# Slot numbers and slot scatters of a mixture-of-experts layer, given out token tile by token tile

## What is computed

```python
def routed_experts(h, idx, w, w_e1, w_e3, w_e2):
    t, d = h.shape
    n = t * TOP_K
    flat_e = idx.reshape(n)
    ...
    order = jnp.argsort(flat_e)
    se, stok, sw = flat_e[order], flat_tok[order], flat_w[order]
    counts = jnp.bincount(flat_e, length=N_EXPERTS)
    padded = (counts + EXPERT_BLOCK - 1) // EXPERT_BLOCK * EXPERT_BLOCK
    ...
    dest = pad_start[se] + (jnp.arange(n) - start[se])
    ...
    xd = jnp.zeros((n_rows, d), h.dtype).at[dest].set(h[stok])
    ...
    return jax.ops.segment_sum(yd * wd[:, None], td, num_segments=t)

def moe_ffn(h, lw):
    scores = jax.nn.sigmoid(h.astype(jnp.float32) @ lw['w_router'].astype(jnp.float32))
    ...
    return routed + swiglu(h, lw['w_s1'], lw['w_s3'], lw['w_s2'])
```

## Time and profile before

| | us |
|---|---|
| median of 3 runs | 1769.77 (1768.54 to 1770.4) |
| the profiled execution | 1767.64, span 1765.8 |
| block A | 776.5 to 876.3 |
| block B | 876.3 to 960.8 |
| TensorE busy | 1562.3 (88% of the span), mean granted clock 0.954 |
| VectorE busy | 1007.9 (57%) |
| ScalarE busy | 728.2 (41%) |
| GpSimd busy | 653.8 (37%) |

### The profile page before, as it was taken

The page is one execution under the profiler, slowest core; times in us unless marked ns, Lnnn a source line. Parts: engine busy times, 40 slices in busy tenths (PEclk is TensorE's granted clock), DMA queues, the critical chain, the costliest instruction groups (busy, mean ns, idle before and its releaser), DMA issues. The chain is left out here.

```text
span 1765.8 us, 22716 instructions
## 1 busy us (share of the span) xinstructions
PE 1562.3 (88%) x7699; PEld 1181.3 (67%) x7699; DVE 1007.9 (57%) x1578; ACT 728.2 (41%) x1067; POOL 653.8 (37%) x727
## 2 busy tenths in 40 slices
PE   7799787788889999999892999999999999999990
PEld 2688687688879998964541666666666666666660
DVE  1956677656665466526552666555555555555644
ACT  2423343333342131102212566555565555656650
POOL 0533474422213332310055345444444444444540
PEclk9999899889989999999896999999999999999995
DMA  9320100000015465444163899999999999999944
GB/s 320 96 93 3 37 1 1 1 1 1 1 47 150 139 204 177 135 148 158 72 263 128 290 357 374 351 344 341 345 348 347 339 344 345 342 332 341 339 149 181
DMA packets 129672, 352.50 MB, mean 200 GB/s; under 512 B 21316, under 2 KB 77256, under 8 KB 102600
## 3 DMA queue, kind: packets, MB, share of 16 engines
q1 hardware_dynamic: 97880, 237.71, 36.9%
q10 hardware_dynamic: 10288, 71.86, 11.1%
q0 software_dynamic: 21440, 42.08, 9.5%
HBM read 335.16 MB, written 47.87 MB: 217 GB/s over the span
## 5 line engine op out<-in xcount | busy, mean ns | idle before, releaser
L2247 DVE TENSOR_TENSOR e_wlo<-mem,e_whi 128x2048 fp32r<-128x2048 f32 x140 | 314.6, 2288 | 119.8 <-ACT e_whi L2187 119.8
L2187 ACT ACTIVATE e_whi<-mem 128x2048 fp32r<-128x2048 f32 x140 | 260.3, 1908 | 36.0 <-PEq L1847 23.6
L2157 PE MATMUL psum<-mem 128*128 128x512 f32 x560 | 252.0, 593 | 1.5 <-ACT mem L2219 1.5
L2137 PE MATMUL psum<-e_whi,e_xhi 128*128 128x512 f32 x560 | 228.2, 407 | 7.1 <-DVE e_xlo L2254 7.1
L2094 POOL TENSOR_TENSOR held<-nhalf 1x1 f32<-1x1 f32 x206 | 126.2, 613 | 284.5 <-DMA sums<-mem_h,si 118.6
L2139 PE MATMUL psum<-e_wlo,e_xhi 128*128 128x512 f32 x560 | 222.3, 397 | 0.0
L2138 PE MATMUL psum<-e_whi,e_xlo 128*128 128x512 f32 x560 | 222.2, 397 | 0.0
L2157 PEld LDWEIGHTS psum<-mem 128*128 128x128 f32 x560 | 101.0, 190 | 102.2 <-issue 102.1
L1481 POOL TENSOR_TENSOR w_lo<-mem,w_hi 128x1024 fp32r<-128x1024 f32 x30 | 76.8, 2581 | 161.3 <-ACT w_hi L1425 161.3
L2254 DVE TENSOR_TENSOR e_xlo<-psum,e_xhi 128x512 fp32r<-128x512 f32 x140 | 90.2, 686 | 77.8 <-ACT e_xhi L2193 77.8
L927 ACT ACTIVATE mem<-psum,small 128x640 f32<-128x640 f32 (+1 forms) x80 | 60.3, 754 | 175.6 <-DVE small L1096 107.2
(11 more groups left out here) (313 smaller groups left out, 3309.5 us busy)
## 6 DMA issues: line engine op xcount, KB each, us to landing
mem<-in_w_e SPq DMA_DIRECT2D x144, 1024.0 KB, 12.4
mem<-in_w_e ACTq DMA_DIRECT2D x66, 1024.0 KB, 11.2
mem<-in_w_mod SPq DMA_DIRECT2D x24, 1024.0 KB, 12.5
mem<-in_w_in SPq DMA_DIRECT2D x16, 512.0 KB, 4.5
mem<-in_w_in SPq DMA_DIRECT2D x3, 2048.0 KB, 8.9
sums<-mem SPq DMA_DIRECT2D x10, 512.0 KB, 16.6
mem<-sums SPq DMA_DIRECT2D x10, 512.0 KB, 7.8
mem<-in_x_sample SPq DMA_DIRECT2D x8, 512.0 KB, 11.4
```

The costliest lines, as they stand in the source:

```text
L2137: pe.matmul(out, xh, wh, start=first, stop=False)
L2157: mm = pe.matmul(pY[:, cs], gT[:, f, :], w2[v][:, f, cs], start=(f == 0), stop=(f == 1))
L2187: act.activation(wHi13[u % 2][:, a], w13[u][:, a], ACT.Copy).then_inc(se["h13"], 1)
L2247: dve.tensor_tensor(wLo13[u][:, a], w13[u][:, a], wHi13[u % 2][:, a].bitcast(F32), ALU.subtract)\
```

## The change

Slot numbers no longer wait for the counts of all tiles. Blocks beyond the first of an expert are given out in the order in which they come up, tile by tile: `over[t]` holds how many such blocks each expert has after t tiles, `cur` where its newest is, `owner` who owns which. Per tile there are now five steps: `place` (TensorE: positions, and counts so far), `blocks_of` (VectorE: which experts need a new block), `ranks` (TensorE: in which order they get one), `new_blocks` (VectorE) and `spread` (TensorE: broadcasts the three columns to all rows), then `slots_of` (VectorE) and `scatter_slots` (GpSimd). For tiles 0 to 2 the numbers are made in block A, and the scatters of tiles 0 and 1 are issued there, between GpSimd's norm steps; tiles 3 and 4 are numbered in B, and tiles 2 to 4 scattered there. The output projection is cut in halves, with `place` between them. In B, SyncE's load of the third expert's second weights (`load_w2(SH - 1)`, 1 MB) moves behind the slot numbers, since their scratch memory lies in that buffer, and ahead of the load of the slot table.

```diff
+    def place(pe, t):
+        pe.wait_ge(s_sel, t + 1)
+        if t:
+            pe.wait_ge(s_k8, 2 * t)
+        for a in range(t + 1):
+            mm = pe.matmul(pPos, tri if a == t else ones, sel[:, a, :], start=(a == 0), stop=(a == t))
+        if t:
+            for a in range(t + 1):
+                mm = pe.matmul(pCnt, sel[:, a, :], ones[:, 0:1], start=(a == 0), stop=(a == t))
+        mm.then_inc(s_pos, 1)
+    def ranks(pe, t):
+        pe.wait_ge(s_bcol, t)
+        pe.matmul(pRank, triX, flag, start=True, stop=False)
+        pe.matmul(pRank, ones[0:NE, 0:NE], over[t], start=False, stop=True).then_inc(s_rank, 1)
+    def spread(pe, t):
+        pe.wait_ge(s_diag, t)
+        pe.matmul(bank(7)[:, 128:128 + 3 * NE], ones[0:NE, :], diag.rearrange("p a e -> p (a e)"),
+                  start=True, stop=True).then_inc(s_bc, 1)
+    def blocks_of(dve, t):
+        chain = Chain(dve, s_rv, route_chain[0])
+        dve.wait_ge(s_pos, t + 1)
+        chain(dve.tensor_scalar(over[t + 1], pCnt, float(P), None, ALU.is_gt))
+        for a in range(2, t + 1):
+            chain(dve.scalar_tensor_tensor(out=over[t + 1], in0=pCnt, scalar=float(P * a), in1=over[t + 1],
+                                           op0=ALU.is_gt, op1=ALU.add))
+        dve.tensor_tensor(flag, over[t + 1], over[t], ALU.subtract).then_inc(s_bcol, 1)
+    def new_blocks(dve, t):
+        dve.wait_ge(s_rank, t)
+        ...
+        for n, v in enumerate((over[t], cur, step1)):
+            ins = dve.tensor_scalar(diag[:, n, :], ident[0:NE, 0:NE], v, None, ALU.mult)
+        ins.then_inc(s_diag, 1)
+        ...
+    def slots_of(dve, t):
+        dve.wait_ge(s_pos, t + 1)
+        if t == 0:
+            dve.wait_ge(s_rec, 16)
+            chain(dve.scalar_tensor_tensor(out=gsel, in0=pPos, scalar=float(NBLK), in1=enum, op0=ALU.mult, op1=ALU.add))
+        else:
+            dve.wait_ge(s_bc, t)
+            ...
+        chain(dve.scalar_tensor_tensor(out=gsel, in0=gsel, scalar=1.0, in1=sel[:, t, :], op0=ALU.add, op1=ALU.mult))
+        chain(dve.max(k8[:, t, :], gsel))
+        ...
+    def scatter_slots(pool, t, part):
+        pool.wait_ge(s_tin, 16)
+        pool.wait_ge(s_k8, 2 * (t + 1))
+        for n in range(t * TOPK + part[0], t * TOPK + part[1]):
+            pool.indirect_dma_start(out=S["slots"], ...
@@ block A, TensorE
             for t in range(1, NT):
-                out_proj(t)
+                out_proj(t, 0)
+                if t >= 2:
+                    place(pe, t - 2)
+                out_proj(t, 1)
+                if t >= 3:
+                    ranks(pe, t - 2)
                 turn(t - 1)
                 router(t - 1)
+                if t >= 3:
+                    spread(pe, t - 2)
@@ block A, GpSimd
                 pool.tensor_tensor(RS2, RS1, nhalf[:, 0:1], ALU.pow).then_inc(sr["rs"], 1)
+                if t == 2:
+                    scatter_slots(pool, 0, (0, 4))
+                if t == 3:
+                    scatter_slots(pool, 0, (4, 8))
+                    scatter_slots(pool, 1, (0, 4))
+                if t == 4:
+                    scatter_slots(pool, 1, (4, 8))
@@ block A, VectorE
                 dve.tensor_tensor(x1[:, t, :], x1[:, t, :], xres[t % 2], ALU.add).then_inc(sr["x"], 1)
+                if t >= 3:
+                    new_blocks(dve, t - 2)
...
                 if 1 <= t < NT - 1:
                     select(dve, t - 1)
+                if t >= 2:
+                    slots_of(dve, t - 2)
+                if 2 <= t < NT - 1:
+                    blocks_of(dve, t - 1)
                 dve.wait_ge(sr["T"], t + 1)
@@ block B, SyncE
                 load_w13(sp, u, u)
-                load_w2(sp, u, u)
+                if u < SH - 1:
+                    load_w2(sp, u, u)
...
+            sp.wait_ge(s_k8, 2 * NT)
+            sp.wait_ge(s_er, 1)
+            load_w2(sp, SH - 1, SH - 1)
             sp.wait_ge(s_tsc, 16 * NT * TOPK)
@@ block B, TensorE (counts, place and block sums of all tiles go)
+            place(pe, 3)
             turn(0)
+            pe.wait_ge(sh["g"], 1)
+            up(1, 0, 2)
+            ranks(pe, 3)
+            up(1, 2, 4)
+            spread(pe, 3)
+            up(1, 4, KT)
+            down(0)
+            turn(1)
+            pe.wait_ge(sh["g"], 2)
+            place(pe, 4)
...
+            pe.wait_ge(s_own, 1)
+            pe.wait_ge(s_k8, 2 * NT)
+            pe.matmul(pOwn, pnum[0:NE, :], owner, start=True, stop=True)
+            pe.matmul(pNb, over[NT], ones[0:NE, 0:1], start=True, stop=True).then_inc(s_er, 1)
+            down(1)
+            turn(2)
@@ block B, VectorE
             dve.memset(xg[1], 0.0).then_inc(s_zero, 1)
+            product(0)
+            blocks_of(dve, 3)
             dve.wait_ge(s_hp, 16 * NT)
             select(dve, NT - 1)
...
+            new_blocks(dve, 3)
+            slots_of(dve, 3)
+            product(1)
+            blocks_of(dve, 4)
+            new_blocks(dve, 4)
+            dve.sem_inc(s_own, 1)
+            slots_of(dve, 4)
             dve.memset(xg[0], 0.0).then_inc(se["z"], 1)
```

More of the change, by code:

```diff
@@ L1591, in up_bank @@
     def up_bank(t):
-        return bank(7 if t == 0 else 0)
+        return bank(2 if t == 0 else 0)
+    RT = M_SC + 7168
+    qv, isn, blkv, gsel = (mem.at(RT + NE * n, NE) for n in range(4))
+    eqb = mem.at(RT + 256, TOPK * NE)
+    diag = mem.at(RT + 256, 3, NE, rows=NE)
+    k8 = mem.at(RT + 768, NT, TOPK)
+    w8 = mem.at(RT + 808, NT, TOPK)
+    owner = mem.at(RT + 848, NE, rows=NE)
+    over = [small[0:NE, 4 + t:5 + t] for t in range(NT + 1)]
+    cur, flag, rank1, step1, mine = (small[0:NE, 10 + n:11 + n] for n in range(5))
@@ L1665, in _, with out_proj @@
             pe.wait_ge(s_wout, 16 * KT)
-            def out_proj(t):
-                if t >= 2:
+            def out_proj(t, half=None):
+                if t >= 2 and half != 1:
                     pe.wait_ge(sr["x"], 2 * (t - 2) + 2)
-                for c in range(2):
+                for c in range(2) if half is None else (half,):
                     for k in range(KT):
@@ L1740, in _ @@
             dve.wait_ge(s_cst, 16)
+            chain = Chain(dve, s_rv, route_chain[0])
+            dve.memset(over[1], 0.0)
+            dve.memset(owner, 0.0)
+            chain(dve.tensor_copy(cur, pnum[0:NE, :]))
+            route_chain[0] = chain.n
             for t in range(NT):
@@ L1874, in turn, with up @@
                 tr.then_inc(sh["T"], 1)
+            def up(t, k0, k1):
+                for k in range(k0, k1):
+                    mm = pe.matmul(up_bank(t).rearrange("p (a n) -> p a n", a=2), h2T[:, k, t * P:(t + 1) * P],
+                                   w13[SH][:, :, k, :], start=(k == 0), stop=(k == KT - 1))
+                if k1 == KT:
+                    mm.then_inc(sh["h"], 1)
             def down(t):
@@ L1938, in _ @@
         def _(pool):
[L1939 to L1946 removed]
+            for t in range(2, NT):
+                scatter_slots(pool, t, (0, TOPK))
             pool.wait_ge(s_tab, 16)
@@ L1977, in _ @@
-            for a in range(2, NT):
-                chain(dve.scalar_tensor_tensor(out=oblk, in0=cnt, scalar=float(P * a), in1=oblk,
-                                               op0=ALU.is_gt, op1=ALU.add))
-            dve.tensor_scalar(oblkb, ones[0:NE, :], oblk, None, ALU.mult).then_inc(s_ob, 1)
-            dve.wait_ge(s_pos, 1)
-            chain(dve.tensor_copy(posv, bank(4)[:, 0:NT * NE].rearrange("p (t e) -> p t e", t=NT)))
-            chain(dve.tensor_scalar(jv, posv, float(P), None, ALU.is_ge))
@@ L1985, in _ @@
-            for a in range(2, NT):
-                chain(dve.scalar_tensor_tensor(out=jv, in0=posv, scalar=float(P * a), in1=jv,
-                                               op0=ALU.is_ge, op1=ALU.add))
-            chain(dve.scalar_tensor_tensor(out=posv, in0=jv, scalar=-float(P), in1=posv, op0=ALU.mult, op1=ALU.add))
-            dve.wait_ge(s_os, 1)
-            chain(dve.tensor_copy(rt[:, 2880:3008], bank(6)[:, 0:2 * NE]))
-            chain(dve.tensor_tensor(ostart, ostart, enum, ALU.subtract))
```

138 lines of the change are left out of this document (50 added, 88 removed).

## The result

The changed kernel takes 1784.82 us (median of 4 runs, 1783.1 to 1785.78) where the kernel before takes 1769.15 beside it (4 runs): a ratio of 1.0087, 95% interval 1.0073 to 1.0102. Slower by 0.9%, 1.5 us under the forecast of 1786.3. Its profiled execution took 1784.27 us (span 1782.5), against 1767.64.

What follows compares the result with a forecast made beforehand. Block B was taken as bound by GpSimd's scatters, block A not. A's +29.0 us less B's 12.5 gave +16.5 us: 1784.1 for the profiled execution, 1786.3 for the median, range 1774 to 1794.

Steps and rivals of the forecast that it cites:

- -12.5 forecast: Block B (slot numbers, slot scatters, shared expert): 12.5 us shorter, bounds 11.7 to 14.7, as the slot table lands earlier.
- +29.0 forecast: Block A (output projection, norm, router, choice of experts): 29.0 us longer from TensorE's stands, added matmuls and lost clock.
- stand at place(0): Middle of out_proj(2) in block A: TensorE waits 2.7 us for tile 0's selection.
- stand at place(1): Middle of out_proj(3) in block A: TensorE waits 6.6 us for tile 0's slot numbers, 17.1 against 10.6.
- stand at place(2): Middle of out_proj(4) in block A: TensorE waits 6.0 us for tile 1's slot numbers, 19.0 against 13.0.
- stands at spread: Behind the router in block A: spread(1) and spread(2) each wait 1.5 us for new_blocks, 3.0 us.
- item 6: Block A: half clock in projection halves behind the three place stands, 5.1 us (bounds 0 to 5.1); spread's stands cost nothing.
- (a): Block A: stands cost no clock, small matmuls run at full clock too; +9.8 us, 1779.6; chance 0.12.
- (b): Fourth turn of block A: scatters hold VectorE up, 3.9 us more; +20.4 us, 1790.2; chance 0.05.
- (c): Block A: the two long stands do not occur, VectorE's chain being quicker; no change, 1768.7; chance 0.08.
- (d): Block A: TensorE stands for no new step, grows 4.0 us by matmuls alone; -8.5 us, 1761.3; chance 0.10.
- (e): Block B: table load waits longer for the shared expert, gain only some 8 us; +21 us, 1790.8; chance 0.05.

Runs made afterwards that it cites:

- table_before_w2: Changed kernel with SyncE loading the slot table ahead of the moved 1 MB weight load: 1783.31 us, ratio 1.0083.
- scatter_in_b: Changed kernel with all 40 scatters issued in block B, slot numbers of tiles 0 to 2 still made in A: 1783.3 us, ratio 1.0088.
- order: Changed kernel with only TensorE's queue reordered: place behind the whole projection, ranks behind the transposition, both spreads moved later: 1759.4 us, ratio 0.9951.
- spread_later: Changed kernel with only the two spreads moved, into out_proj(4) and the shared expert's first product: 1785.33 us, ratio 1.0091.
- early_release: Changed kernel with place waiting only for VectorE's last read of the PSUM bank, not for the slot numbers: 1775.79 us, ratio 1.0042.
- before_again: The kernel before, unchanged, traced a second time: 1780.99 us, beside runs where the kernel before took 1781.33.
- all_scatters_b: The kernel of order_table_early with all 40 scatters issued in block B: 1781.97 us, ratio 0.9997; run again 1780.26 us, ratio 0.9994.
- order_table_early: The kernel of order with SyncE's table load and moved weight load ahead of the stores of tiles 2 and 3: 1753.9 us, ratio 0.9917.
- before_waits: The kernel before with only three TensorE waits for the selection added, in the middle of out_proj(2), (3) and (4): 1775.92 us, ratio 1.0038.

## Why the prediction was right, and where it was not

**B (-12.5 forecast, -13.1 measured).** The steps held one by one: the scatters ended 16 us before the load (17 forecast), the load was issued 56.1 us into B (56.5), it took 2.8 us longer than before (the forecast left 0 to about 3 open and took 2.4; `table_before_w2` puts 1.95 of it on the weight load), and the gathers behind it were unchanged. The drain, costed as before, was 0.65 us shorter, which is why B gained 13.1 and not 12.5. Which part brings the gain was left unsaid: `scatter_in_b` shows that it is the slot numbers done early, and not the sixteen scatters.

**A (+29.0 forecast, +31.4 measured).** By term, from the TensorE rows above:

| us | forecast | measured |
|---|---|---|
| stand at place(0) | 2.7 | 1.06 |
| stand at place(1) | 6.6 | 6.52 |
| stand at place(2) | 6.0 | 4.48 |
| stands at spread | 3.0 | 2.49 |
| matmuls of place, ranks, spread | 5.6 | 6.3 |
| clock | 5.1 | 7.2 |
| joins and the first turn of A | 0 | 3.4 |

place(1) was right because its chain was: from the end of out_proj(2) to the slot numbers the trace gives 823.74 to 840.92, 17.2 us, and I had 17.1. place(0) and place(2) were mis-sized for the same reason, TensorE being late by itself: the first half ahead of place(0) took 8.46 instead of 7.08, and the half ahead of place(2) 8.47. What TensorE loses to the clock ahead of a wait it gets back at the wait: in the trace of `table_before_w2` the half ahead of place(2) takes 9.87 and the stand is 2.98, together 12.85, where the kernel after has 8.47 + 4.48 = 12.95.

The step that failed is item 6, the clock, which came out at 7.2 us, above its bound of 5.1. Its three falls of 1.7 us were to follow the stands at place; instead the stand of 1.06 us cost nothing, the two long ones 2.4 each, and the 1.24 and 1.25 us stands, "which I leave at nothing", 1.4 each, with another 1.4 ahead of place(0): 8.9 us, less the 1.7 that the kernel before pays at the start of A. Rows 9 had stands of 0.85 us that cost nothing, and I carried that to 1.5 us without a row between. `order` and `spread_later` show that these falls go with the stands: where the stands are gone, the halves behind take 7.1 us. The size is not fixed by the stand, though: behind the same 1.24 or 1.25 us other traces have 10.00 (`early_release`) and 9.87 and 9.97 (`table_before_w2`).

The last line is what the sum had no term for: TensorE's first turn waits 0.92 and 1.59 us there (VectorE and ScalarE, unrelated lines) where it waited 0.83 before; with a slower router that makes 2.2 us. Of these 1.5 stand in the second trace of the kernel before too, so they vary from one execution to the next and are not a cost of the change; against that trace A grew by 30.1. Some 0.2 us are lost at each of the five places where new steps stand between old ones. The two over-forecast stands and these small losses cancel, so the total is closer than its terms, and that closeness is luck.

**Rivals.** (a) fell: the clock is at 0.50 behind every stand but the shortest. (b), VectorE held up by scatters, fell in its direction. The pair met, but GpSimd was the one that waited. The timeline of VectorE and GpSimd of the kernel after, and then the instructions of line 1681, the compare steps:

```profile
858.72 1.28 DVE L1885 SCALAR_TENSOR_TENSOR mem<-mem,small 128x1024 f32<-128x1024 f32 x1 [0.66 <-POOL small L1847]
...
858.84 2.10 POOL L1694 DMA_INDIRECT slots<-mem  x1 [0.21 <-issue]
...
894.23 0.69 DVE L1681 TENSOR_TENSOR mem<-mem 128x512 f32<-128x512 f32 x1
...
894.56 1.20 POOL L1694 DMA_INDIRECT slots<-mem  x1 [0.30 <-issue]
```

```profile
L1681 DVE TENSOR_TENSOR mem<-mem x5: 691/693/693, 838.5 to 931.3; 128x512 f32<-128x512 f32 x5
```

VectorE's step started 0.12 us earlier and keeps its 1.28 us; the scatter takes 2.10 instead of 0.97, 1.1 more, about what was left of VectorE's step. It happens once in each of two turns, off the path, and the last scatter of A takes 1.20 us, started inside a compare step that ended at 894.92. That it is not the first scatter of a row that is slow shows in `order`: there one in the middle of a row, started at 867.02 inside VectorE's residual step of 866.72 to 867.94, takes 1.76 us. In all of these the scatter ends 0.84 to 0.94 us after VectorE's step. The Trainium skill, "SBUF — State Buffer", section "Who interferes with whom", states that a VectorE instruction with two SBUF inputs and a GpSimd instruction that reads SBUF exclude each other and that whoever issues first keeps the ports. These rows agree with it: the order of issue decides who pays, which I had not weighed. The compare steps themselves (line 1681, before) stay at 691 to 693 ns. Why did the kernel before show nothing, with 40 scatters beside them? Where one of its scatters started inside a compare step, at most 0.08 us of that step was left (900.80 and 900.83, for one), or both started together (898.25 and 898.26). So the earlier trace rows were weaker evidence than I took them for: they show where the scatters fell, and not that the two engines leave each other alone. (c) and (d) did not occur in this kernel, but `order` is (d) made to happen: A grew by 6.9 us, under the 9 us that (d) named as its point of decision, and the result was a gain of 9.4 us, where (d) had 8.5. (e) fell, B gained 13.1.

The drain at the end of A ended at 897.7, 1.9 us after the last scatter and 6.4 before VectorE, so it cost nothing, as costed.

## What to carry to other kernels

A step split off from a later block goes into an in-order queue behind the work that doesn't need it, at the place where its input is there by the trace; count the longest chain of the other engine to that place before writing the order. The same steps cost 31 us in one order and 7 in the other. Look then at what queue ends the block, and move what follows the shortened chain (here one table load) out from behind copies that it does not need. And ask what a wait is for: here more than half of a wait for slot numbers (6.4 of 11.0 us) was a wait for a PSUM bank that had been read by then.

## What the hardware showed that was not expected

- What a stand of TensorE costs in clock, by the half projection behind it (7.08 us at full clock). Inside a projection: nothing after 1.05 to 1.12 us; 1.75 us after 2.1 us; 1.9 to 2.6 us after 3.0 to 7.6 us, longer stands not costing more. Behind a router, which has waits of its own: 1.3 to 2.9 us after 1.24 and 1.25 us. The same stand does not cost the same in every trace. After the 0.52 us at the end of a projection in `order` the clock stayed at 1.00.
- In block B of `before_again`, `all_scatters_b` and `all_scatters_b_2` VectorE or ScalarE stood for 12 to 29 us at a time beside an unbroken stream of 32 to 40 scatters, with no instruction named as releaser. The DMA engines were 7% busy over the first such wait of `before_again` (910 to 938 us); in `all_scatters_b_2` they were busy at its start and idle over its last 10 us. Both traces of `order_table_early`, one taken beside `all_scatters_b_2`, where B has 24 scatters in three groups, don't show it, nor do the first trace of the kernel before and those of `before_waits` and `scatter_in_b`, where 40 go in a row. The kernel before took 1780 to 1781 us beside the kernels that show it and 1769 beside the others, which fits its B of 97.1 against 84.5. The cause is open.
- A small indirect scatter started inside a VectorE step with two SBUF inputs ended 0.84 to 0.94 us after that step (2.10, 1.76 and 1.20 us instead of 0.97), and VectorE's step took no longer. How much a scatter loses thus depends on how much of the step is left when it starts.
